# Front of a conditioned decoder step: later modulation blocks behind the output rounds, one bias product a block, injections copied by ScalarE, rows loaded by two queues

## The reference, cut to what matters

```python
def split_mod(c, w, b, n):
    mod = jnp.einsum("bd,de->be", jax.nn.silu(c), w) + b
    return jnp.split(mod, n, axis=-1)

def s5_mixer(u, h0_re, h0_im, a_re, a_im, log_dt, b_re, b_im, c_re, c_im, d_skip, w_glu):
    ...
    bu = jnp.einsum("blgp,gnp->blgn", uf.astype(jnp.complex64), b_bar)
    bu = bu.at[:, 0].add(lam_bar * h0)
    a_seq = jnp.broadcast_to(lam_bar, bu.shape)
    _, h = lax.associative_scan(_linear_combine, (a_seq, bu), axis=1)
    y = jnp.real(jnp.einsum("blgn,gpn->blgp", h, c_mat)) + d_skip.astype(f32).reshape(SSM_GROUPS, SSM_GROUP) * uf
    z = jax.nn.gelu(y.reshape(bsz, length, D_MODEL))
    a, g = jnp.split(z @ w_glu.astype(f32), 2, axis=-1)
    out = (a * jax.nn.sigmoid(g)).astype(u.dtype)
```

## Time and profile before

| what | us |
|---|---|
| median of three runs | 3435.63 |
| lowest and highest run | 3426.26, 3446.24 |
| span of the profiled execution | 3430.0 |
| median of the runs less that span | 5.6 |
| first output round starts, ends (last one) | 235.9, 266.6 |
| gated unit starts | 275.7 |
| first PEER tile's transposes start | 312.5 |

### The profile page before, as it was taken

How to read it: one execution, slowest core, us unless ns; L and a number is a source line. 1 busy time by engine, 2 the same in 40 slices (tenths; PEclk the granted TensorE clock), 3 DMA queues, 4 the chain that set the end, 5 groups by cost and what they waited for, 6 DMA issues and landing times.

```text
span 3430.0 us, 62993 instructions
## 1 busy us (share of the span) xinstructions
PE 2541.4 (74%) x25173; PEld 935.2 (27%) x25173; DVE 2329.2 (68%) x5485; ACT 1302.1 (38%) x4056; POOL 1277.8 (37%) x1133
## 2 busy tenths in 40 slices
PE   4878997868668766668878887878587677666665
PEld 3756322323003200112235452224132032001000
DVE  8753885897866776465553458776888867764655
ACT  3441333333333333344433225553443343333333
POOL 0010343444444444433411227563444444443442
PEclk8979998878667766778999898888787787667667
DMA  9966999999999999999955369999999999999997
GB/s 325 348 241 267 398 413 414 415 403 411 426 426 414 413 426 424 410 420 399 395 180 235 118 227 371 355 411 412 394 421 410 426 421 414 423 425 385 424 426 318
DMA packets 178977, 1284.73 MB, mean 375 GB/s; under 512 B 22264, under 2 KB 23264, under 8 KB 30744
## 3 DMA queue, kind: packets, MB, share of 16 engines
q0 software_dynamic: 151696, 1109.99, 79.0%
q1 hardware_dynamic: 26416, 170.18, 13.1%
q10 hardware_dynamic: 576, 0.59, 0.0%
HBM read 1268.49 MB, written 12.18 MB: 373 GB/s over the span
## 4 chain that ended last, share of the span: by engine, by line
PE 36%; DMA 34%; DVE 19%; ACT 6%; issue 3%; POOL 1%; SPq 0%; another core or an unknown queue 0%; DVEq 0%; ACTq 0%; PEldq 0%; POOLq 0%
DMA arena<-peer_uv,arena 31%; PE psum L2948 13%; DVE arena L2315 9%; PE psum L2875 6%; PE psum L2834 3%; PE psum L3355 2%; DMA arena<-b_mod 2%; PE psum L3106 1%; PE psum L3037 1%; DVE arena L2225 1%; ACT arena L1604 1%; ACT arena L1601 1%; DVE arena L2329 1%; PE psum L2702 1%; DVE arena L1891 1%
## 5 line engine op out<-in xcount | busy, mean ns | idle before, releaser
L2948 PE MATMUL psum<-arena 32*32 32x512 f32 x16384 | 1470.3, 791 | 720.7 <-ACT arena L1604 652.3
L1267 POOL DMA_INDIRECT arena<-peer_uv,arena x1040 | 1160.5, 1116 | 1703.0 <-PE psum L2948 1482.7
L2315 DVE SCALAR_TENSOR_TENSOR arena<-arena 128x1024 f32<-128x1024 f32 x1040 | 1273.5, 1228 | 687.8 <-DMA arena<-peer_uv,arena 670.3
L1591 ACT ACTIVATE arena<-arena 128x1 f32<-128x1 f32 x944 | 190.9, 202 | 1390.8 <-DVE arena L2315 1383.4
L2948 PEld LDWEIGHTS psum<-arena 32*32 32x32 f32 x16384 | 215.8, 117 | 1799.3 <-ACT arena L1604 1584.5
L1604 ACT ACTIVATE arena<-arena 128x32 f32<-128x32 f32 x928 | 298.2, 321 | 30.3
L1601 ACT ACTIVATE arena<-arena 128x1 f32<-128x1 f32 x944 | 277.8, 294 | 30.7
L2875 PEld LDWEIGHTS psum<-arena 128*128 128x128 f32 x2048 | 241.5, 195 | 68.6 <-issue 66.9
L2875 PE MATMUL psum<-arena 128*128 128x128 f32 x2048 | 258.8, 282 | 1.1 <-ACT arena L1528 1.1
L2834 PE MATMUL psum<-arena 128*128 128x512 f32 x256 | 126.0, 625 | 3.2 <-ACT arena L1488 2.4
L2702 PE MATMUL psum<-arena 128*9 128x128 f32 x2048 | 78.8, 317 | 58.4 <-DMA arena<-b_mod 58.3
(11 more groups left out here) (352 smaller groups left out, 2430.8 us busy)
## 6 DMA issues: line engine op xcount, KB each, us to landing
arena<-w_mod SPq DMA_DIRECT2D x64, 1024.0 KB
arena<-peer_wq SPq DMA_DIRECT2D x16, 2048.0 KB, 11.4
arena<-peer_uv,arena POOLq DMA_INDIRECT x1040
arena<-w_glu SPq DMA_DIRECT2D x5, 2048.0 KB, 7.3
arena<-mod_rows SPq DMA_DIRECT2D x5, 1024.0 KB
arena<-w_o SPq DMA_DIRECT2D x1, 4096.0 KB
arena<-x_after_layer SPq DMA_DIRECT2D x7, 512.0 KB
arena<-mod_rows SPq DMA_DIRECT2D x6, 512.0 KB
```

The source lines that it names most:

```text
L1267: pool.indirect_dma_start(ring[r], None, a[f"peer_uv{t // 5}"], bass.IndirectOffsetOnAxis(ap=ix, axis=0)).then_inc(landed[r], 16)
L1591: act.activation(col, col, ACT.Gelu_apprx_tanh).then_inc(s_gl, 1)
L2315: dve.scalar_tensor_tensor(out=u, in0=u, scalar=GELU_IN if beside_exps(t, m) else 1.0, in1=h, op0=ALU.mult, op1=ALU.mult, accum_out=at(DOT ...
L2948: ins = pe.matmul(acc_of(t, i, c), diag[rows, r, :], ring[r][rows, D + 512 * c:D + 512 * (c + 1)], start=(m == 0), stop=last, skip_group_c ...
```

## The change

- Buffers: MOD_PLACES gives each block its places by hand. Blocks 0 to 14 have four places of 2 MB between them; blocks 15 to 26 have five halves (three, X, and the two of H); 27 to 31 have places of their own. A half is loaded when its last reader, found by last_use, is done.
- Order: blocks 25 to 29 stand behind output rounds 0, 2 and 3, blocks 30 and 31 behind the gated unit of the first tile. Blocks 18 to 24 stand behind "t" round 3, blocks 15 to 17 behind "t" rounds 0 to 2.
- Rounds: "u" in eight halves; the four "k" rounds become one with 64 products, to which d_skip is added as a diagonal, so that the skip product and the final additions of VectorE go; "t" writes whole columns out of padded kernels, and is copied by one instruction instead of four.
- Bias: one product of four rows ahead of each block in place of four behind it.
- Engines: ScalarE copies the injections (VectorE only half of round 3) and half of the states, and applies Gelu straight from PSUM; VectorE loses the skip product, the copies and the additions.
- Queues: half of the prompt rows and the reads of blocks 0 to 3 go out on ScalarE's queue; the rates of the S5 layer are loaded first by themselves.

```diff
-        MOD_AFTER = [("m", 0), ("m", 1), ("s", 0), ("u", 0), ("u", 1), ("u", 2), ("u", 3), ("k", 0),
-                     ("m", 2), ("i", 1), ("k", 1), ("m", 3), ("i", 2), ("k", 2), ("i", 3), ("k", 3)]
-        MOD_BEHIND = (0, 1, 3)
+        MODS_BEHIND = {("m", 0): (6,), ("m", 1): (7,), ("s", 0): (8,), ("u", 7): (9,), ("m", 2): (10,), ("m", 3): (11,),
+                       ("i", 3): (12, 13), ("k", 0): (14,), ("t", 0): (15,), ("t", 1): (16,), ("t", 2): (17,),
+                       ("t", 3): (18, 19, 20, 21, 22, 23, 24), ("y", 0): (25, 26), ("y", 2): (27, 28),
+                       ("y", 3): (MOD_TURN,)}
...
+        MOD_PLACES = [T01, T23, MC, MH, T01, T23, MC, T01, T23, MJ, MG, T01, T23, MH, T01, X01, MH, X20, X12, MH, X01, X20,
+                      MH, X12, X01, X20, X12, MR, MJ, ML, MW, MS_]
...
+                if n >= DEEP:
+                    sp.wait_ge(s_modmm[n % 2], mods_done(n - DEEP))
+                k = 0
+                for piece in MOD_PLACES[n]:
+                    before = last_use(n, piece)
+                    if before and before[0] > n - DEEP:
+                        sp.wait_ge(s_modmm[before[0] % 2], mods_done(before[0]) - 1 + before[1])
...
+            sp.wait_ge(s_mm, round_no[("u", 2 * NR - 1)] + 1)
+            for n in range(13, 15):
+                mod_load(n)
+            sp.wait_ge(s_mm, round_no[("i", NR - 1)] + 1)
+            for n in range(15, 27):
+                mod_load(n)
...
+            sp.wait_ge(s_hx, HX_PIECES)
+            for n in range(27, MOD_NORM[0]):
+                mod_load(n)
...
+            act.dma_start(at(CL, 4 * D, 64, P), a["x_prompt"].rearrange("(c s j) d -> s c (j d)", s=2, j=TC // 2)[1]
+                          ).then_inc(s_x5, 16)
...
+            for b in range(2):
+                act.wait_ge(s_modst[b], 16 * (MOD_S5 // 2))
+            act.dma_start(mod_s, mod_dram[0:1, 0:D].partition_broadcast(P)).then_inc(s_mods5, 16)
...
+            def injections(r):
+
+                pieces = [piece for k in range(1 if r == NR - 1 else 2) for gp in range(2) for piece in injected(r, k, gp)]
...
+                    ins = act.activation(toep.rearrange("p (r g) m -> p r g m", r=NR)[:, :, 4 * r:4 * r + 4, :],
+                                         ps.rearrange("p r (g m) -> p r g m", g=4), ACT.Copy)
...
+                    act.activation(
+                        z5[64 * s:64 * s + 64, :, RG * GP * r:RG * GP * (r + 1)].rearrange("p j (g q) -> p j g q", g=RG),
+                        ps[0:64, :, 4 * s:4 * s + 4, :].rearrange("p g j q -> p j g q"), ACT.Gelu_apprx_tanh
+                    ).then_inc(s_gelu, 1)
...
-                for s in range(2):
-                    yv = h5[64 * s:64 * s + 64, RG * r:RG * (r + 1)]
-                    tt(yv, yv, ps[0:64, :, 4 * s:4 * s + 4, :], ALU.add)
...
+                pe.matmul(out, at(EYE4, P, 0, 4), mod_bias(n), start=True, stop=False,
+                          skip_group_check=True)
...
-                            ins = pe.matmul(out[:, :, t0:P], at(EYE - GP * odd, 32, 32 * r, 32 * r + GP),
-                                            ksb[r][:, 4 * n_:4 * n_ + 4, 0:P - t0], start=(odd == 0), stop=(odd == 1),
-                                            skip_group_check=True)
+                            ins = pe.matmul(ps[32 * c:32 * c + 32, r, :].rearrange("p (g m) -> p g m", g=4),
+                                            at(EYE - GP * odd, 32, 32 * r, 32 * r + GP),
+                                            ksb[32 * r:32 * r + GP, 4 * n_:4 * n_ + 4, PAD - t0:PAD - t0 + P],
+                                            start=(odd == 0), stop=(odd == 1), skip_group_check=True)
...
+            def kernels(ps):
+
+                for gl in range(RG):
+                    bank, slot = divmod(gl, 4)
+                    for r in range(NR):
+                        g = RG * r + gl
+                        pe.matmul(ps[32 * r:32 * r + GP, bank, P * slot:P * (slot + 1)], bk[:, g, :],
+                                  cl[:, g, 0:TC, :], start=(slot == 0), stop=False, skip_group_check=True)
```

More of the change, by code:

```diff
@@ L280, in wait_copied @@
+        copied = {key: n + 1 for n, key in enumerate(ROUNDS)}
         def wait_copied(eng, key):
-            who, n = copied[key]
-            eng.wait_ge(s_evA if who == "A" else s_evV, n)
+            eng.wait_ge(s_evA, copied[key])
+            if key == ("i", NR - 1):
+                eng.wait_ge(s_evV, 1)
         def half_of(key):
             kind, r = key
-            return r % 2 if kind == "y" else int(kind in "is")
+            return r % 2 if kind == "y" else int(kind == "s" or kind == "i" and r < 3)
@@ L289, in half @@
         def half(key):
             return psum[:, 4 * half_of(key):4 * half_of(key) + 4, :]
-        def round_before(no):
-            mine = [key for key in ROUNDS[:no] if half_of(key) == half_of(ROUNDS[no])]
-            return mine[-1] if mine else None
-        def mods_between(key):
-            return [divmod(MOD_FIRST + n, 2) for n, after in enumerate(MOD_AFTER) if after == key]
-        def pairs(eng, first, last, pair):
-            if first == 0:
-                for b in range(2):
-                    pair(0, b, True)
-            with eng.Fori(first // 2 + (first == 0), last // 2) as i:
-                for b in range(2):
-                    pair(i, b)
@@ L311, in program, with segment @@
         NSEG = 4
         SEG = CH // NSEG
+        SCANNED = [2 + 5 * (SEG - 1) + 2 * s for s in range(NSEG)]
+        def segment(s):
+            return slice(0 if s == 0 else SEG * s + 1, min(SEG * (s + 1) + 1, CH))
         assert 4 * HALF * NSEG + HALF * NB <= ARENA - MS - D and 2 * SEG * HALF <= D
@@ new lines, in loads_of @@
+            def loads_of(n):
+                return 16 * sum(len(MOD_PLACES[m]) + 1 for m in range(n % DEEP, n + 1, DEEP))
+            for n in range(MOD_S5):
+                mod_load(n)
+            sp.dma_start(at(CL, 4 * D, 0, 64), a["x_prompt"].rearrange("(c s j) d -> s c (j d)", s=2, j=TC // 2)[0]
+                         ).then_inc(s_x5, 16)
+            sp.dma_start(at(XS, D, 0, NB), a["x_sample"]).then_inc(s_x5, 16)
+            sp.dma_start(at(GBC, D), a["g_norm"][0:1, :].partition_broadcast(P)).then_inc(s_mods5, 16)
@@ L1471, in _ @@
[L1471 to L1474 removed]
+                if key == ("t", NR - 1):
+                    break
+                for m in MODS_BEHIND.get(key, ()):
+                    mod_copy(m)
+            behind = MODS_BEHIND[("t", NR - 1)]
+            for s in range(2):
+                act.wait_ge(s_scan, SCANNED[s])
+                for gp in range(2):
+                    for k in range(2):
+                        act.activation(hxv[64 * k:64 * k + 64, gp, :, segment(s)],
+                                       hpv[64 * gp:64 * gp + 64, k, :, segment(s)], ACT.Copy).then_inc(s_hx, 1)
+                for m in behind[3 * s:3 * s + 3]:
+                    mod_copy(m)
@@ L2074, in _ @@
                 tt(dst_im, dst_im, part, ALU.add)
-            for r in range(1, NR):
-                injections(r)
+            dve.wait_ge(s_mm, round_no[("i", NR - 1)] + 1)
+            pieces = [piece for gp in range(2) for piece in injected(NR - 1, 1, gp)]
+            for out, src in pieces[:-1]:
+                link(dve.tensor_copy(out, src))
+            dve.tensor_copy(*pieces[-1]).then_inc(s_evV, 1)
             wait_copied(dve, ("i", NR - 1))
-            dve.wait_ge(s_mm, round_no[("k", NR - 1)] + 1)
+            dve.wait_ge(s_modmm[0], mods_done(10))
             link(dve.memset(hpx[:, 0, :], 0.0))
```

585 lines of the change are left out of this document (304 added, 281 removed), and 3 rows, old and new, of the table BANKS_FREE.

## The result

| | before | after |
|---|---|---|
| median of nine runs each, us | 3431.47 | 3408.12 |
| lowest and highest, us | 3418.0, 3446.24 | 3398.88, 3418.2 |
| profiled span, us | 3430.0 | 3406.0 |

The ratio is 0.9929, 95% interval 0.991 to 0.9948: 23 us faster, against 20 forecast. The forecast of 3416 counted from 3435.6, the median of three runs; nine runs of the same kernel give 3431.5, so 4 of the 8 us between 3416 and 3408 lie there. Not every step on the way was right; two errors of 5 to 8 us stand against each other.

A forecast was written before the change was run, and what follows sets the result against it. DMA engines bound the kernel, with about 40 us of empty DMA time in the front. Output rounds 34 us earlier, less 14 of blocks and waits, gave 20 us: 3435.6 - 20 = 3416 us, range 3390 to 3441.

The forecast's parts named there:

- B table at 59; input rows 75; u to 91.5: Early chain ahead of the scan: VectorE ends B table at 59 us, input rows at 75; ScalarE ends "u" at 91.5.
- Queues: Stored-row wait moved to ScalarE costs nothing if squares come by 52 us; prompt rows on a second queue bring no bandwidth.
- Injection copies 7.0 us a round: ScalarE's 16 copies per injection round ahead of the scan take 7.0 us, with ends 4.6 and 8.5.
- the 5 that I had named as a sign against me: Injection rounds: the forecast is wrong if ScalarE's 16 copies take under 5 or over 9 us.
- t0 at 140, rounds of 4.4, t3 ends 166: TensorE's response rounds: first starts at 140 us, each takes 4.4, the fourth ends at 166 with three blocks between.
- Block transfer 5.45, share over 0.9: Stream of 2 MB blocks before the output rounds: 5.45 us each, 6.5 blocks; DMA share over 0.9 from 165 us on.
- Output rounds 202, their end 247, gated unit 256, first tile 293: End of the front: output rounds 202 to 247 us, gated unit at 256 (19.6 earlier), first tile's transposes at 293.
- Bounds: Injections 8 better, 5 worse; responses 6, 12; half-clock blocks 20 worse; transfer 3, 2; all good 3392, all bad 3440 to 3450.
- Rival A: Front overlap holds better: output rounds at about 188, gated unit near 240, 35 us earlier, 3400 us; chance 0.20.
- Rival B: Block waits of 3 us and more bring mid-front TensorE to half clock, costing 7 to 20 us: 3430; chance 0.18.
- Rival C: Clock stays at 1.2 GHz from first output round through the gated unit: 41 us slower, 3476; chance 0.07.
- the rule weighed there: Trainium skill on HAM oscillation: loop pieces start cold after DMA waits; by it each of blocks 18 to 29 would.

The follow-up runs named there:

- e3: Against the change: ScalarE squares the x rows before waiting for stored rows and issuing the modulation reads, instead of behind them; 3406.3 us.
- e11: Against the change: four bias products a block in place of one, and second half of the prompt rows issued by SyncE behind block 3; 3405.5 us.
- e7: Against the change: 11.6 us of extra VectorE work (a clear and 11 products) ahead of the scan; 3407.6 us.
- e5: Against the change: one more half buffer, from the scan's scratch, for blocks 21, 24 and 25; 3389.7 us, ratio 0.9895.
- e2: Against the change: blocks 15 to 18 each multiplied one round earlier; 3408.9 us.
- e9: Against the change: extra half buffer, squares ahead of the reads, blocks 15 to 18 a round earlier with sample states copied before block 24's rows; 3387.45 us, ratio 0.9852.
- e1: The change again, unaltered, for a second profile; 3408.08 us, ratio 0.993 to the kernel before.
- e6: Against the change: 48 added products of 9 x 128 columns behind each of blocks 18 to 23, into an unread bank; 3458.2 us.

## Why the prediction was right, and which steps were not

- *B table at 59; input rows 75; u to 91.5*: 65.6, 80.8 and 96.5, 5 to 6 us late. The step that failed is **Queues**: "cost nothing while the squares come by 52 us". They ended at 58.2. The cover was counted, what pushes against it was not: blocks 2 and 3 were stored late because the first blocks came late, and ScalarE's squares stood behind that wait. e3 shows the order (table at 58.9), e11 the start (block 0 7 us earlier, table at 59.1). And "brings no bandwidth" was true, but I asked only what the queue gives, not what the transfer does to the weights beside it: at half rate it cost 5 to 7 us of them (e11).
- *Injection copies 7.0 us a round*: 4.8 (4.61 and 0.18), near the lower end 4.6 and under the 5 that I had named as a sign against me. VectorE's row was the wrong neighbour; ScalarE's contiguous rate was the right one. 3.5 rounds times 2.2 are 7.7 us. So i3 ended at 122.1 (forecast 122) and the scan started at 125.8 (129): the two errors cancelled, by luck.
- *t0 at 140, rounds of 4.4, t3 ends 166*: 138.8, 3.93 (4.84 the first), 162.0. Right within 4 us.
- *Block transfer 5.45, share over 0.9*: the pitch was 6.0 at a share of 0.83. Over 6.5 blocks that is 3.6 us more than forecast. From the end of block 17's product (158.2, forecast 161) to the output rounds it took 45.8 us in place of 41, which ate what t3 had won. Right in kind, as e7 (scan: slack) and e5 (space: 15.5 us) show; the term was sized by a transfer alone, while a loop of product, release, issue and transfer goes through two and a half buffers.
- *Output rounds 202, their end 247, gated unit 256, first tile 293*: 204.0, 248.4, 256.9, 293.7; the wait for block 26 was 4.5 for 3.5. VectorE idle from 183: from 179.3 to 253.0. Query weights: no wait. DMA share under 0.7 from 100 to 160 us: 0.56 and 0.53, with 0.82 between. That the gated unit hit within 1 us is luck in part: the same program had it at 267.4 in its other profile.
- *Bounds*: the good ends listed add up to 17 us (3399, not 3392), the bad ones to 39 (3455, not 3440 to 3450). The range took neither sum; it was set by A and B.
- *Rival A* (output rounds at 188) needed space and an earlier table: e5 alone comes to 195.2, with the edits of e3 and e2 (e9) to 189.2, and the granted clock from 164 to 204 us was 0.79 and 0.87 there, not full. *Rival B*'s slow response rounds are there, in e1's profile, at a price of 10 us, without the waits that it gave as their cause. *Rival C* did not come: 0.95 over the output rounds, 14.00 us for each two units of the gated unit. By the rule weighed there each of blocks 18 to 29 would start cold; six of the twelve did (five of the seven ahead of the output rounds, and block 26).

## What to carry to other kernels

When loads turn through a few buffers, take the time per load from the whole loop (transfer, product, release, issue), and try one half buffer more before anything else: here it was worth 15 us of front, where the whole rebuilding had won 19. A wait moved to another engine costs what stands behind it there; put independent work ahead of it. And read GB/s beside the DMA share: loads into half of the partitions show 0.9 and more at half the rate, so put them behind what is urgent.

## What the runs showed of the hardware

- One program had a response round at 2.4 GHz in one profile and at 1.2 in another (3.93 and 7.37 us), in a stretch where TensorE was not idle for more than 1.2 us at a time; the gated unit came 10 us later. What brought the clock down is not shown.
- A 9x128 product took 0.06 us where four PSUM partition groups were written in turn (blocks) and 0.22 where only one was (e6), as much as one that writes 72 partitions.
- ScalarE copied 64x384 with gaps from PSUM at 4.8 us for 16 copies, VectorE at 6.8.
- While a load into 64 partitions was on its way, all loads together ran at 182 to 233 GB/s at a DMA share of 0.91 to 1.01; without one they had 415 to 427.
